# Plain one-hot rows of the gate matrix: from VectorE to ScalarE

## The reference, cut to what matters

```
v1, i1 = top_k(s1, 16);  v2, i2 = top_k(s2, 16)       # per token and head, 8 heads
sc, ci = top_k(v1[:, None] + v2[None, :], 16)
e1 = i1[ci // 16];  e2 = i2[ci % 16];  experts = e1 * 128 + e2
gate = softmax(sc)
act = gelu(u_table[experts] . x)
out = sum(gate * act * v_table[experts])
```

## Time and profile before

| | us |
|---|---|
| median of 3 executions | 4653.38 |
| lowest, highest | 4643.26, 4664.34 |
| the profiled execution, its own time | 4646.84 |
| its span in the trace | 4645.1 |
| the gate matrix stage in it | 2218 to 2457 |

### The profile page before, as it was taken

The page is one execution under the profiler, slowest core; times in us unless marked ns, Lnnn a source line. Parts: engine busy times, 40 slices in busy tenths (PEclk is TensorE's granted clock), DMA queues, the critical chain, the costliest instruction groups (busy, mean ns, idle before and its releaser), DMA issues.

```text
span 4645.1 us, 71896 instructions
## 1 busy us (share of the span) xinstructions
PE 4319.6 (93%) x26508; PEld 4144.1 (89%) x26508; DVE 2683.9 (58%) x4808; ACT 1060.3 (23%) x1861; POOL 2586.4 (56%) x1653
## 2 busy tenths in 40 slices
PE   8999999999989997985888999999999999999997
PEld 8999888878889996985878999999999999999996
DVE  1000233344442314898896777777777777777776
ACT  1000122222221102101223222222223222223223
POOL 4455322222235453443335777877777878777783
PEclk9999999999999999997999999999999999999998
DMA  5222322322233221111447999999999999999994
GB/s 199 99 100 95 118 109 102 111 88 78 78 136 121 100 95 54 63 63 56 172 158 287 362 366 366 399 398 402 398 392 377 396 387 406 394 396 400 386 411 199
DMA packets 265977, 1082.02 MB, mean 233 GB/s; under 512 B 24496, under 2 KB 89136, under 8 KB 181168
## 3 DMA queue, kind: packets, MB, share of 16 engines
q0 software_dynamic: 74736, 544.24, 28.7%
q1 hardware_dynamic: 87840, 388.01, 22.6%
q10 hardware_dynamic: 103328, 148.96, 9.4%
HBM read 1019.65 MB, written 66.85 MB: 234 GB/s over the span
## 4 chain that ended last, share of the span: by engine, by line
PE 60%; DVE 12%; POOL 10%; DMA 8%; issue 7%; ACT 1%; ACTq 0%; DVEq 0%; POOLq 0%
PE banks L461 29%; PE banks L703 12%; PE banks L639 11%; POOL w_lo L356 7%; POOL work L384 2%; DMA work<-in_v_rows,idx_all 2%; DMA work<-in_u_rows,idx_all 2%; PE banks L530 2%; PE banks L492 1%; PE banks L691 1%; DMA work<-early_act 1%; DVE work L1404 1%; DMA rows_own<-in_v_rows,idx_all 1%; PE banks L500 1%; DVE mv_hi L1403 1%
## 5 line engine op out<-in xcount | busy, mean ns | idle before, releaser
L356 POOL TENSOR_TENSOR w_lo<-w_raw,w_hi 128x1024 fp32r<-128x1024 f32 x480 | 1154.6, 2406 | 414.2 <-ACT w_hi L1024 409.7
L362 POOL TENSOR_SCALAR w_hi<-w_raw 128x2048 fp32r<-128x2048 f32 x130 | 253.1, 1947 | 1475.7 <-PE banks L461 1269.0
L461 PE MATMUL banks<-mv_hi,w_hi 128*128 128x256 f32 x3648 | 863.5, 318 | 62.1 <-DVE mv_lo L1150 37.5
L461 PE MATMUL banks<-mv_lo,w_hi 128*128 128x256 f32 x3648 | 836.2, 311 | 0.0
L461 PE MATMUL banks<-mv_hi,w_lo 128*128 128x256 f32 x3648 | 835.1, 310 | 0.0
L703 PE MATMUL banks<-mv_hi,w_hi 128*128 128x384 f32 x2048 | 704.2, 344 | 92.9 <-DVE work L1443 82.7
L461 PEld LDWEIGHTS banks<-mv_hi,w_hi 128*128 128x128 f32 x3648 | 652.3, 189 | 125.9 <-issue 102.5
L1024 ACT ACTIVATE w_hi<-w_raw 128x1024 fp32r<-128x1024 f32 x480 | 507.5, 1060 | 998.6 <-PE banks L703 741.8
L639 PE MATMUL banks<-mv_hi,w_hi 128*128 128x384 f32 x2048 | 695.8, 340 | 15.2 <-POOL w_lo L356 11.5
L703 PE MATMUL banks<-mv_hi,w_lo 128*128 128x384 f32 x2048 | 697.2, 340 | 0.0
L703 PE MATMUL banks<-mv_lo,w_hi 128*128 128x384 f32 x2048 | 697.2, 340 | 0.0
(11 more groups left out here) (155 smaller groups left out, 4788.2 us busy)
## 6 DMA issues: line engine op xcount, KB each, us to landing
w_raw<-in_wstream SPq DMA_DIRECT2D x480, 512.0 KB, 7.9
w_raw<-in_wstream SPq DMA_DIRECT2D x130, 1024.0 KB, 4.8
gate_matrix<-work ACTq DMA_DIRECT2D x12, 2048.0 KB, 6.3
work<-gate_matrix ACTq DMA_DIRECT2D x32, 768.0 KB, 15.6
out_p<-work ACTq DMA_DIRECT2D x34, 320.0 KB, 2.2
work<-out_p ACTq DMA_DIRECT2D x34, 320.0 KB, 3.4
gate_scratch<-work ACTq DMA_DIRECT2D x32, 320.0 KB, 2.2
work<-gate_scratch ACTq DMA_DIRECT2D x16, 640.0 KB, 3.9
```

What stands on the lines that cost most here:

```text
L356: pool.tensor_tensor(w_lo[s][:, part], raw[s][:, part], w_hi[s][:, part].bitcast(f32), ALU.subtract) \
L362: pool.tensor_scalar(w_hi[s][:, :], raw[s][:, :], 1.0, 0.0, ALU.mult, ALU.add).then_inc(hi_done, 1)
L461: last = pe.matmul(acc(dst, h), a[s][:, P * k:P * k + P], b[h][:, k, :], start=(k == k_first and n == 0), stop=(k == k_last and n == 2))
```

## The change

The rows of `oh2` are made by ScalarE in two steps: Abs of (index - iota) for four tokens into a new buffer `oh_far`, then one Relu of (1 - distance) over all four, which is 1 where the distance is 0 and 0 elsewhere. VectorE keeps the rows of `oh1`. ScalarE makes the rows of the next round before it copies the bank of the present one; the last trip of its loop is written out apart, so that it doesn't make rows past the end. TensorE waits for `oh2_ready` too.

```
+        oh_far = sb("oh_far", [P, 4 * KEYS])
+        oh_dist, oh2_ready = sem("oh_dist"), sem("oh2_ready")
...
                     pe.wait_ge(oh_ready, 16 * i + q + 1)
+                    pe.wait_ge(oh2_ready, 16 * i + q + 1)
                     pe.wait_ge(g_evac, 16 * i + q + 1)
...
             act.sem_inc(g_evac, 2)
-            with act.Fori(0, GBLK // 2) as i:
+
+            def one_hot(i, q):
+
+                if q:
+                    act.wait_ge(oh2_ready, 16 * i + q)
+                for t in range(4):
+                    last = act.activation(oh_far[:, KEYS * t:KEYS * t + KEYS], iota, ACT.Abs, scale=-1.0,
+                                          bias=pick_t[2][:, ds(2 * GT * i + 4 * q + t, 1)])
+                last.then_inc(oh_dist, 1)
+                act.wait_ge(oh_dist, 16 * i + q + 1)
+                at = 4 * (q % 2)
+                act.activation(oh2[:, at:at + 4, :].rearrange("p t e -> p (t e)"), oh_far[:, :], ACT.Relu, scale=-1.0,
+                               bias=ones[:, 0:1]).then_inc(oh2_ready, 1)
+
+            def gate_trip(i, final):
                 for q in range(2 * GT // 4):
                     w, qq = q // 8, q % 8
+                    if q < 2 * GT // 4 - 1 or not final:
+                        one_hot(i, q + 1)
                     act.wait_ge(g_full, 16 * i + q + 3)
...
+            act.wait_ge(nat_ready, 2)
+            one_hot(0, 0)
+            with act.Fori(0, GBLK // 2 - 1) as i:
+                gate_trip(i, False)
+            gate_trip(GBLK // 2 - 1, True)
...
                         tok = ds(2 * GT * i + 4 * q + t, 1)
-                        dve.tensor_scalar(oh2[:, n, :], iota, pick_t[2][:, tok], None, ALU.is_equal)
                         last = dve.tensor_scalar(oh1[:, n, :], iota, pick_t[1][:, tok], pick_t[0][:, tok],
                                                  ALU.is_equal, ALU.mult)
```

## The result

| | before | after |
|---|---|---|
| median of 6 executions, us | 4649.59 | 4669.99 |
| lowest, highest | 4643.26, 4664.34 | 4661.90, 4680.85 |
| ratio, with its 95% interval | | 1.0037 (1.0021 to 1.0053) |
| the profiled execution | 4646.84 | 4669.54 |
| its span | 4645.1 | 4667.7 |

The kernel is 0.37% slower: a loss that six executions tell from zero, and that stays inside the 0.5% which the prediction called no change.

A forecast was written before the change was run, and what follows sets the result against it. TensorE was taken to set the pace, interrupted when GpSimd's splits slow VectorE; afterwards ScalarE binds. 96 x 2.41 = 231.4 plus 23.9, less 2.0, plus 0.7 gives 254.0 us against 238.5, so median 4669, range 4625 to 4705.

The forecast's parts named there:

- The round: ScalarE's list per round in the gate stage: four Abs, wait, Relu and copy, 2.41 us, above TensorE's 1.94.
- the two bounds: ScalarE's wait for the last Abs before Relu: 0.04 us from VectorE's self-wait taken, 0.18 from ScalarE's store kept for range.
- The handovers: ScalarE's waits and store issues after copy and Gelu, once per eight rounds: 0.80 us each, beside Gelu's 0.39.
- The splits: GpSimd's ten weight splits in the stage slow VectorE and stop TensorE; the change hides them, removing 53 us.
- the prediction's two grounds: Why splits are hidden: ScalarE's 1.99 us of other work delays TensorE's need; TensorE's delay up to 1.4 us goes unnoticed.
- The stage: Making of the gate matrix: 96 rounds of 2.41 us plus ScalarE's other work, 254.0 us against 238.5.
- TensorE's waits would be named after ScalarE's Relu: Sign of being right: TensorE's waits in the gate stage carry ScalarE's Relu, not VectorE's gated rows.
- the clock as a rival: TensorE's clock falls to 0.50 for a fifth of the rounds, adding 28 us, median 4697; chance 0.04.
- ScalarE does not keep up: Rival that ScalarE keeps up: round 1.82 us, deciding below 2.25; stage 36 us less, median 4617; chance 0.12.
- it is not much slower: Rival of a much slower ScalarE: no overlap, round 3.10 us, stage 82 us more, median 4735; chance 0.13.
- the splits no longer stop TensorE: Rival that splits still stop TensorE: up to 2 us in each of ten, +20 on the forecast, 4689; chance 0.06.
- no table load: Rival that ScalarE reloads tables: two loads of 1.283 us at each of 12 Gelus, 31 us more, 4700; chance 0.03.

The follow-up runs named there:

- experiment 2: Changed kernel with both stores issued behind the four Abs and rows made one round further ahead: stage 236.3 us, 4648.85 us, ratio 0.9982 to before.
- Experiment 1: Both kernels with the stage's ten GpSimd weight splits cut to 16 of 2048 columns: stage 238.5 to 187.4 us in before, 255.2 to 254.9 in after.
- experiment 3: Changed kernel with ScalarE making plain rows of two of four tokens, VectorE the rest: stage 249.0 us, 4663.08 us, ratio 1.0011 to before.
- experiment 5: Changed kernel, late stores; ScalarE makes three of four tokens (two or four rounds' stock) or two (four rounds): ratios 0.9976, 0.9894, 0.9912 to before.
- Experiment 6: Kernel before with VectorE's row instruction at 129 elements, read as 3 x 43, ScalarE's stage work untouched: stage 221.1 us, 4634.88 us, ratio 0.9956.
- three of four tokens, two rounds: Changed kernel, late stores, ScalarE making plain rows of three of four tokens, two rounds in stock: stage 226.2 us, 4642.93 us, ratio 0.9976 to before.
- experiment 4: Changed kernel with plain rows shared two and two and ten GpSimd splits cut to 16 of 2048 columns: stage 198.8 us, 4617.02 us.
- experiment 7: Changed kernel with plain rows shared two and two, late stores and VectorE's 3 x 43 form: stage 189.0 us, 4600.79 us, ratio 0.9880 to before.
- three of four with four rounds: Changed kernel, late stores, ScalarE making plain rows of three of four tokens, four rounds in stock: stage 198.3 us, 4609.56 us, ratio 0.9894 to before.
- before without splits: Kernel before with the stage's ten GpSimd weight splits cut to 16 of 2048 columns: stage 187.4 us, 4603.23 us in all.

## Why the prediction was right

The forecast was 4669 us within 4625 to 4705, no change the likeliest; measured, 4669.99. That the two agree to 1 us is luck: the forecast stands on a median before of 4653.4, which is 4649.6 over six executions, and on a growth of 15.5 us where the medians differ by 20.4. What the working earned is the stage, 254.0 against 255.2.

**The round.** The sum said 2.41 us, and the timeline has 2.41. Its terms are near, partly by cancelling: Abs 0.391 for 0.387, its step 0.29 for 0.29, Relu 0.724 for 0.715, copy 0.578 for 0.599. The bare wait ahead of Relu is 2239.48 - (2238.18 + 1.27) = 0.03 us; the 0.04 of VectorE's row was the right one of the two bounds, not the 0.18 of the store.

**The handovers.** 0.69 + 0.10 of overlap lost is 0.79 behind the copy, 0.66 + 0.10 = 0.76 behind the Gelu, against 0.80 each. Eleven of each lie ahead of the last copy, 17.1 us, and with the 1.6 us at the trips' ends (below, under the stage) that is 18.7; experiment 2, which hides them, brought 18.9. The Gelu's own 0.39 stays in both.

**The splits.** Experiment 1 is the test: the same edit is worth 51 us on before and 0.3 on after. Of the prediction's two grounds the first carried it alone: ScalarE's other work falls in just these rounds and puts TensorE's wish later, so that VectorE's rows were ready 0.8 us or more ahead of the products in every split. The second, a delay of up to 1.4 us that ScalarE wouldn't notice, was not drawn on in after; where the table has TensorE wait 1.0 and 1.4 us for VectorE, it waited for the Relu.

**The stage.** Expected 254.0, or +15.5; measured 255.2, +16.7. A term was left out: the 1.07 us at the end of a loop trip where 0.66 was counted, four times (4.2 us in the table of waits), 0.4 us more each; the fifth, ahead of the trip that is written out apart, has 0.69. That is 1.6 us, against a miss of 1.2; the handovers, priced 0.6 us too high in all, go the other way.

**The whole.** The profiled execution grew by 22.7 us, the stage by 16.7. The stage starts 0.8 us later (2219.1 for 2218.3), and the other 5.2 us lie behind it, in one pair of executions, where the six of before alone are spread over 21 us. The medians of six differ by 20.4 us. Whether the change costs anything outside its stage stays open; no experiment was made for it.

**What was wrong.** The text said that TensorE's waits would be named after ScalarE's Relu. They appear as issue or under VectorE's name. And it counted the clock as a rival only for pauses in each round. The clock did fall to 0.50, three times, each time behind one of the five stops of 2.2 to 2.6 us at the trips' ends. The chain behind one of them has 1.33 and 1.92 us where quiet rounds have 1.13 and 1.05:

```profile
2266.29 1.33 PE banks L694 x8
2267.62 1.92 PE banks L641 x6
```

It cost next to nothing there, for TensorE has time in hand: ScalarE's next Relus are 2.50 us apart instead of 2.41 once behind each, 0.3 us in all. In before the same thing stood four times, behind waits of 1.8 to 2.0 us, and experiments 3 and 5 show its price where TensorE has no time in hand, so it is a part of the 51 us that the change removed: TensorE's waits but the first account for 40.8 - 1.5 = 39.3 of them, and the rest lies in groups that took longer. The rivals are out: ScalarE does not keep up (2.41, not under 2.25), it is not much slower, the splits no longer stop TensorE (experiment 1), and no table load is in the stage.

**Where the gain went.** The change took away 51 us (experiment 1) of stop. It put in (2.41 - 1.95) x 96 = 44 us of ScalarE's pace and some 23 us of its stores, Gelus and trip ends (18.7 + 4.3). The difference is the loss.

## What to carry to other kernels

When work moves to an idle engine, add up that engine's whole list, bare waits and store issues included, against the pace of the engine that it feeds; a store that was issued behind queued work cost nothing here, one that was issued behind a bare wait cost 0.8 us. Share a load in the proportion in which both engines keep up, rather than move it, and give the buffers enough stock for the longest interruption, because a stop of TensorE of 3.3 us was paid for nearly twice in experiment 3. Read who ended a wait from the times, by the constant distance to the instruction that really came last, before the table's name is believed. And ask first whether the interruption can be avoided where it arises: another shape of the same instruction brought 20 us with no row moved to another engine.

## What the runs showed of the hardware

- A VectorE tensor_scalar of 128 elements in a plain row takes 0.28 or 0.34 us when GpSimd rests and up to 2.1 when it works; without the splits the longest plain row was 0.44 us. With 129 elements, read as 3 x 43, it takes 0.33 to 0.44 us, and no GpSimd instruction held it up in 96 rounds. The Trainium skill (VectorE: DVE Perf Modes, What auto-detection actually checks) says that the mode which uses both ports needs outermost dimensions of source and destination that are both even or equal, and (SBUF — State Buffer, Who interferes with whom) that in this mode the two engines block each other. Experiment 6 agrees with both; that the port is the cause is the page's statement, the run shows only the times.
- Behind a stop of 3.3 us TensorE's granted clock was 0.50 over the window of 4.4 us shown, and the next three groups took 2.6 us more than they do at full clock. The fall came behind all ten stops of 3.2 to 3.3 us in experiment 3, behind six of ten of 2.4 to 2.5 us (three of four tokens, two rounds), behind three of five of 2.2 to 2.6 us in after, and in before behind four waits of 1.8 to 2.0 us but behind none of its six of 2.6 to 2.8 us. Experiment 6 has one, behind its first wait of 2.0 us. In the kernels whose longest wait in the stage was at most 1.6 us (experiments 2, 4 and 7, three of four with four rounds, before without splits) it stayed at 1.00. So the length of the last stop alone doesn't tell; what does, no run here shows.
- On ScalarE the copy out of the bank took 0.57 to 0.58 us where it starts 0.1 us ahead of the end of the activation before it (92 of 96 in after), and 0.60 us where it starts behind a wait or later (the other four, and all 96 in before): the same line and shape, so it is how the copy follows, not what it copies.
- The end of a loop trip cost ScalarE 0.4 us more behind the bare wait for the Gelu (1.04 to 1.07 us of idle time for 0.66, four times in after). In experiment 2, where four Abs and a Relu lie between the Gelu and the end of the trip, ScalarE has no idle time there.
